# PEER of a one-core decoder layer: the u part first, then v in quarter-feature tiles, with 80 gathered tokens

## The reference, cut to what matters

```
s_top, i_top = lax.top_k(s, PEER_TOPK)                  # per head and half key
best_s, pos = lax.top_k(cand_s, PEER_TOPK)
idx  = ...                                              # (ntok, 128) experts of 16384
gate = softmax(best_s)                                  # (ntok, 128)
act  = gelu(einsum('nd,ned->ne', x, u[idx])) * gate
out  = einsum('ne,ned->nd', act, v[idx])
x    = x + g_c * out ; y = adaLN(RMSNorm(x), c)
```

## Time and profile before

| | us |
|---|---|
| median of 3 runs (lowest, highest) | 2712.4 (2710.21, 2713.03) |
| the profiled execution | 2713.36 |
| its span | 2711.5 |
| busy PE / PEld / DVE / ACT / POOL | 2600.9 / 2400.8 / 1361.7 / 960.9 / 1522.9 |
| HBM read / written | 558.8 / 24.5 MB |

### The profile page before, as it was taken

The page is one execution under the profiler, slowest core; times in us unless marked ns, Lnnn a source line. Parts: engine busy times, 40 slices in busy tenths (PEclk is TensorE's granted clock), DMA queues, the critical chain, the costliest instruction groups (busy, mean ns, idle before and its releaser), DMA issues.

```text
span 2711.5 us, 58935 instructions
## 1 busy us (share of the span) xinstructions
PE 2600.9 (96%) x24221; PEld 2400.8 (89%) x24221; DVE 1361.7 (50%) x2384; ACT 960.9 (35%) x1378; POOL 1522.9 (56%) x724
## 2 busy tenths in 40 slices
PE   5899999889979999999999999999999999999997
PEld 3799999557758999999999988999989999988887
DVE  0540355863236556994576376200676002666566
ACT  1333333341223434444333333333333333333334
POOL 0366676023125776887555544777445776667653
PEclk9899999889978999999999999999999999999999
DMA  9977744587764443445555655555655555888873
GB/s 375 391 282 273 277 158 159 189 286 239 245 221 159 172 164 132 169 155 165 179 188 172 190 185 191 193 183 179 196 186 196 190 180 197 300 324 311 302 272 113
DMA packets 182466, 585.57 MB, mean 216 GB/s; under 512 B 30104, under 2 KB 41000, under 8 KB 153512
## 3 DMA queue, kind: packets, MB, share of 16 engines
q1 hardware_dynamic: 141640, 509.69, 53.6%
q0 software_dynamic: 14672, 55.59, 5.5%
q10 hardware_dynamic: 26000, 18.06, 2.3%
HBM read 558.80 MB, written 24.50 MB: 215 GB/s over the span
## 4 chain that ended last, share of the span: by engine, by line
PE 74%; issue 12%; POOL 10%; DVE 3%; DMA 1%; ACT 0%; POOLq 0%; DVEq 0%; ACTq 0%; SPq 0%
PE bank L905 74%; POOL ring_lo L777 8%; POOL staged L881 1%; POOL ring_lo L784 1%; DVE staged L2860 1%; DMA staged<-late_acts,staged 0%; PE bank L908 0%; DMA staged<-in_w_ada 0%; DVE staged L2336 0%; POOL staged L874 0%; ACT hi_peer L1702 0%; DVE staged L2360 0%; ACT staged L1702 0%; DVE staged L2393 0%; DVE staged L2906 0%
## 5 line engine op out<-in xcount | busy, mean ns | idle before, releaser
L1702 ACT ACTIVATE hi_peer<-kept 128x1024 fp32r<-128x1024 f32 x544 | 546.2, 1052 | 1070.0 <-PE bank L905 1070.0
L777 POOL TENSOR_TENSOR ring_lo<-kept,hi_peer 128x1024 fp32r<-128x1024 f32 x288 | 720.4, 2525 | 279.0 <-ACT hi_peer L1702 279.0
L905 PE MATMUL bank<-h_hi,ring_lo 128*128 128x288 f32 x2848 | 838.0, 294 | 0.0
L905 PE MATMUL bank<-act_hl,hi_peer 128*128 128x248 f32 (+1 forms) x3072 | 706.4, 316 | 4.3 <-POOL ring_lo L784 2.2
L905 PE MATMUL bank<-h_hi,hi_peer 128*128 128x288 f32 x2048 | 608.8, 297 | 2.8 <-POOL ring_lo L777 2.6
L905 PE MATMUL bank<-h_lo,hi_peer 128*128 128x288 f32 x2048 | 604.2, 295 | 0.0
L905 PE MATMUL bank<-act_hl,ring_lo 128*128 128x248 f32 x2048 | 565.4, 276 | 0.0
L905 PEld LDWEIGHTS bank<-act_hl,hi_peer 128*128 128x128 f32 x3072 | 501.7, 188 | 64.5 <-issue 18.9
L905 PEld LDWEIGHTS bank<-h_hi,ring_lo 128*128 128x128 f32 x2848 | 536.6, 188 | 0.0
L784 POOL TENSOR_TENSOR ring_lo<-kept,hi_peer 128x1024 fp32r<-128x1024 f32 (+1 forms) x128 | 264.5, 2066 | 280.0 <-ACT hi_peer L1702 279.3
L905 PE MATMUL bank<-staged 64*64 64x64 f32 (+10 forms) x6520 | 364.4, 284 | 27.5 <-issue 20.0
(11 more groups left out here) (262 smaller groups left out, 2967.3 us busy)
## 6 DMA issues: line engine op xcount, KB each, us to landing
kept<-in_peer_u SPq DMA_DIRECT2D x128, 1024.0 KB, 4.8
kept<-in_peer_v SPq DMA_DIRECT2D x128, 1024.0 KB, 5.7
kept<-in_w_ada SPq DMA_DIRECT2D x64, 1024.0 KB, 8.8
kept<-in_w_in SPq DMA_DIRECT2D x50, 1024.0 KB, 4.8
staged<-in_w_ada SPq DMA_DIRECT2D x32, 1024.0 KB, 6.5
kept<-in_w_adaf SPq DMA_DIRECT2D x32, 1024.0 KB, 5.5
kept<-in_w_out SPq DMA_DIRECT2D x16, 1024.0 KB, 4.8
kept<-in_w_q SPq DMA_DIRECT2D x16, 1024.0 KB, 4.8
```

What stands on the lines that cost most here:

```text
L777: pool.tensor_tensor(ring_lo[:, n % RING_SLOTS, cols], ring[n % RING_SLOTS][:, cols], hi_slot(n)[:, cols].bitcast(F32), ALU.subtract).then ...
L905: return pe.matmul(out, lhsT, rhs, start=start, stop=stop)
L1702: return act.activation(out, in_, ACT.Copy)
```

## The change

The v part comes after all of u, as 128 tiles of four values of b and a quarter of the features (512), in four passes of 8 tiles per quarter; the quarters come in the order 2, 3, 0, 1. `GATHERED` is 80, `VN` 208, and the 40 steps are spread over the 128 tiles. Banks 4 to 7 hold a pass's four 128-feature blocks, each with 2 x 208 columns, so all v tiles have two matmuls per block (416 and 208 columns). GpSimd makes 1024 columns of low weights in every tile and VectorE the other 1024; the cast of the activations moves from VectorE to ScalarE, in two parts of 2 x 208 columns; the first half of a high slot is free at `half_used`. Activations are two buffers of 32 x 208 and one of 32 x 80 for the gathered tokens (`late`), so a u tile has two gelus; `acts` of quarters 0 and 1 are spilled to DRAM and loaded back for the last two. Gates are made for 208 tokens, 52 groups. A pass ends with VectorE's `take_pass`, 8 instructions.

```diff
-GATHERED = 40
+GATHERED = 80
 VN = N - GATHERED
...
+GATE_REST = [min(3, GATE_LAST - at) for at in range(0, GATE_LAST, 3)]
+GATE_TILES = 4 * GATE_BODIES + len(GATE_REST)
+GATE_GROUPS = 12 * GATE_BODIES + GATE_LAST
...
+        segments = [("u", 0), ("u", 1), ("u", 2), ("u", 3), ("v", 2), ("v", 3), ("v", 0), ("v", 1)]
         n_end = n_p + len(segments) * SEG
-        n_v2 = n_p + 6 * SEG
+        n_late = n_p + 4 * SEG
+        LATE_TILES = 4 * SEG
+        V_ORDER = [q for what, q in segments[4:]]
+        PASSES, PASS = 4, SEG // 4
 
...
         def gathered_after(step):
 
-            return 9 + step * 45 // (STEPS - 1)
+            return 9 + step * (LATE_TILES - 19) // (STEPS - 1)
 
...
-        acts = [words(M_ACTS + b * QUARTER * N, QUARTER, N) for b in range(2)]
+        acts = [words(M_ACTS + b * QUARTER * N, QUARTER, VN) for b in range(2)]
+        late = words(M_ACTS + QUARTER * VN, QUARTER, GATHERED)
+        acts_spill = nc.dram_tensor("acts_spill", (2, P, QUARTER, VN), F32, kind="Internal").ap()
...
+
+            def load_acts(q, t):
+
+                own = slice(4 * t, 4 * t + 4)
+                sp.dma_start(acts[q][:, own, :], acts_spill[q][:, own, :]).then_inc(S(f"beside{q}_landed"), 16)
+
+            for m in range(LATE_TILES):
+                n = n_late + m
+                q, at, t = v_place(m)
+                src = v_dram[q * QUARTER + 4 * t:q * QUARTER + 4 * t + 4, :, at * 512:(at + 1) * 512]
+                sp.wait_ge(used, n - RING_SLOTS + 1)
+                sp.dma_start(ring[n % RING_SLOTS].rearrange("p (b d) -> p b d", b=4),
+                             src.rearrange("b a d -> a b d")).then_inc(landed[n % RING_SLOTS], 16)
+                if gates3_at(m + 2) is not None:
+                    load_gates(3, 0, gates3_at(m + 2))
+                if m == SEG:
+                    sp.wait_ge(S("aux_moved"), AUX_MOVED + 32)
+                for b in range(2):
+                    if at == 1 and m // SEG == 1 + b:
+                        if t == 0:
+                            sp.wait_ge(S("acts_split"), 2 * SEG * (1 + b))
+                        load_acts(b, t)
 
...
-            for s, (what, q) in enumerate(segments[:6]):
-                if what == "u":
-                    lo_tiles(n_p + s * SEG, SEG)
-                    continue
-                with pool.Fori(0, SEG // RING_SLOTS) as i:
-                    for j in range(RING_SLOTS):
-                        lo_front(n_p + s * SEG + j, i)
+            for s in range(4):
+                lo_tiles(n_p + s * SEG, SEG)
             v_halves = T["peer_v"].rearrange("e (h d) -> (e h) d", h=2)
-            for m in range(2 * SEG):
-                lo_front(n_v2 + m)
+            for m in range(LATE_TILES):
+                lo_front(n_late + m)
                 if m == 2:
...
 
                 def u_tile(i, j):
                     pe.wait_ge(S("gelu_done"), i * 4 + (q * SEG + j + 1))
-                    if q >= 2:
-                        pe.wait_ge(S("out_taken"), 16 * (q - 1) - 8 + j + 1)
                     dense(n0 + j, h2_hi, h2_lo, i, j)
 
                 if q == 1:
...
+            def v_tile(m):
+
+                first, last = m % PASS == 0, m % PASS == PASS - 1
                 both = first or last
+                turns = [(dt, e) for dt in range(4) for e in range(4)] if both else \
+                    [(dt, e) for e in range(4) for dt in range(4)]
+                pe.wait_ge(S("lo_ready"), lo_halves(n) + 1)
+                pe.wait_ge(S("acts_split"), 2 * m + (2 if both else 1))
                 for dt, e in turns:
+                    if not both and (dt, e) == (0, 2):
+                        pe.wait_ge(S("acts_split"), 2 * m + 2)
+                    if first and e == 0 and m:
+                        pe.wait_ge(S("out_taken"), 4 * (m // PASS - 1) + dt + 1)
+                    cols = slice((e * 4 + dt) * P, (e * 4 + dt + 1) * P)
+                    hi_lo, out = act_hl[:, slot, e, :], ps[4 + dt]
+                    matmul(out[:, 0:2 * VN], w_hi[:, cols], hi_lo, first and e == 0, False)
+                    mm = matmul(out[:, 0:VN], w_lo[:, cols], hi_lo[:, 0:VN], False, last and e == 3)
+                    if last and e == 3 and dt < 3:
...
+            def late_hi(m, part):
+
+                n = n_late + m
+                if m >= 2:
+                    if part == 0:
+                        act.wait_ge(S("half_used"), m - 1)
+                    else:
+                        act.wait_ge(used, n - 1)
+                if part == 0:
+                    act.wait_ge(landed[n % RING_SLOTS], (n // RING_SLOTS + 1) * 16)
+                cols = slice(part * D // 2, (part + 1) * D // 2)
+                copy(hi_slot(n)[:, cols], ring[n % RING_SLOTS][:, cols]).then_inc(S("hi_ready"), 1)
+                late_acts_hi(m, part)
+
+            def late_acts_hi(m, part):
+
+                if part == 0 and m % SEG == 0:
+                    if m < 2 * SEG:
+                        act.wait_ge(S("gates_applied"), 8 * V_ORDER[m // SEG] + 2)
+                    else:
...
+                def tile(i, j, begin=False):
                     act.wait_ge(used, i * 4 + (n0 + j + 1))
+                    hi(n0 + j + 2, i)
+                    if begin:
+                        act.wait_ge(S("side_moved"), 16 + 16 * q)
+                        if q >= 2:
+                            act.wait_ge(S("aux_moved"), AUX_MOVED + 16 * (q - 1))
+                    at = bass.ds(i * 4 + j, 1)
+                    activate(acts[q % 2][:, at, :].rearrange("p o n -> p (o n)"), ps[j % 4][:, 0:VN], ACT.Gelu)
+                    activate(late[:, at, :].rearrange("p o n -> p (o n)"), ps[j % 4][:, VN:N], ACT.Gelu
+                             ).then_inc(S("gelu_done"), 1)
+
+                def spill(b):
+
+                    act.dma_start(acts_spill[b], acts[b]).then_inc(S("aux_moved"), 16)
...
+            def split_acts(m, part):
+
+                n = n_late + m
+                lo, hi = (act_hl[:, n % 2, 2 * part:2 * part + 2, c * VN:(c + 1) * VN] for c in (1, 0))
+                dve.wait_ge(S("acts_hi"), 2 * m + part + 1)
+                ins = tt(lo, acts_part(m, part), hi.bitcast(F32), ALU.subtract)
+                if part == 0:
+                    ins.then_inc(S("acts_split"), 1)
+                    return
                 cols = slice(D // 2, D)
+                dve.wait_ge(S("hi_ready"), 2 * dense_index(n) + part + 1)
                 tt(ring_lo[:, n % RING_SLOTS, cols], ring[n % RING_SLOTS][:, cols], hi_slot(n)[:, cols].bitcast(F32),
+                   ALU.subtract).then_inc(S("acts_split"), 1)
...
+            def take_pass(p):
+
+                for dt in range(4):
+                    k_ = 4 * p + dt
+                    if k_:
+                        dve.wait_ge(S("out_taken"), k_)
+                    if dt < 3:
+                        dve.wait_ge(S("v_sum"), 3 * p + dt + 1)
                     else:
...
+
+            for m in range(LATE_TILES):
+                if m >= 2 * SEG and m % SEG == 0:
+                    dve.wait_ge(S(f"beside{V_ORDER[m // SEG]}_landed"), EARLY_LANDED + 16 * PASS)
+                for side in range(2):
+                    split_acts(m, side)
+                if m == 1:
+                    dve.wait_ge(S("gelu_done"), 4 * SEG + 4)
+                    link(dve.memset(spread_acts, 0.0))
+                late_work(m)
+                if gates3_at(m) is not None:
+                    apply_gates(3, gates3_at(m) // 2, gates3_at(m) % 2)
+                if m and m % PASS == 0:
+                    take_pass(m // PASS - 1)
+            link(stt(out=gain3, in0=mods[:, SC_F], scalar=1.0, in1=over(prm("gfin"), 2, NS), op0=ALU.add, op1=ALU.mult))
+            dve.sem_inc(S("final_step"), 1)
+            take_pass(LATE_TILES // PASS - 1)
```

More of the change, by code:

```diff
@@ L520, in dense_index, with v_place, acts_part, gates3_at @@
             return n - n_z if n < n_ada1 else n - n_wo + 50
[L522 to L525 removed]
+        def v_place(m):
+            return V_ORDER[m // SEG], m % SEG // PASS, m % PASS
+        def acts_part(m, part):
+            q, _, t = v_place(m)
+            return acts[q % 2][:, 4 * t + 2 * part:4 * t + 2 * part + 2, :]
+        def gates3_at(m):
+            return (m - 2) // 3 if m % 3 == 2 and m < 24 else None
         def hi_slot(n):
@@ new lines, in _ @@
+                    spill(1)
+                    with act.Fori(SEG // 4 - 2, SEG // 4) as i:
+                        for j in range(4):
+                            tile(i, j)
+                else:
+                    for j in range(4):
+                        tile(0, j, j == 0)
+                    with act.Fori(1, SEG // 4 - 1) as i:
+                        for j in range(4):
+                            tile(i, j)
+                    for j in range(4):
+                        tile(SEG // 4 - 1, j)
+                        if j >= 2:
+                            for part in range(2):
+                                late_acts_hi(j - 2, part)
```

(1 more changed line is left out.)

360 lines of the change are left out of this document (114 added, 246 removed).

## The result

| | before | after |
|---|---|---|
| median, us (lowest, highest) | 2712.7 (2710.21, 2713.03) | 2779.7 (2766.74, 2787.93) |
| profiled execution, us | 2713.36 | 2766.74 |
| its span, us | 2711.5 | 2764.9 |
| span from the start of v work to the end of it, us | 755.9 (four windows) | 816.8 |

The changed kernel takes 1.0243 of the time before, 95% interval 1.0223 to 1.0262: 2.4% slower, where 0.6% faster was forecast. (The median before is that of four executions.) The profiled execution is the fastest of the four of the changed kernel ("after" from here on), so the profile shows 13 us less than the median.

The account below looks back on a forecast made before the run. TensorE, 98 to 100% busy, was taken as the bound. 2711.5 span - 9.1 gates - 755.9 old v + 698.3 new v + 42 GpSimd + 6 pass ends + 3 gate products = 2695.8, giving 2697 us; range 2668 to 2728.

Parts of the forecast that it names:

- The gates: u quarter making gate products: 52 instead of 62 groups at 0.91 us each, -9.1 us.
- TensorE's own v time: v part: 614.4 dense tiles (4.80 each) + 80.4 steps + 3.5 `turn_late` = 698.3 us, against 755.9 before.
- the rival of hidden loads: Dense v tiles: 208-column matmuls take 0.097 us, tile 4.56; total 2681, or 2670 with stalls at lower bound; chance 0.18.
- The sign named for it: Late v tile: next matmul 0.112 us after a 208-column one starts, or 0.097 if loads are hidden.
- u quarters 2 and 3, ScalarE's two gelus, spills, tail: u part and end: u quarters stay 204.8 us; gelus, spills, reloads cost 0; tail the same length.
- VectorE's part: v part: 6 us for takes at pass boundaries plus 3 for quarter 3's gate products; work per tile less than before.
- the pass ends: 15 pass boundaries: VectorE's takes from PSUM delay TensorE 0.4 us each, 6 us, bounds 0 and 22.
- Late weights: v tile loads in 2 KB pieces land late; at 0.4 us per step the gain is gone, 2712; chance 0.12.
- GpSimd's stalls: v part: low weights late behind gathers, 2.1 us per pair of steps, 20 pairs, 42 us; bounds 22 and 142.
- its break-even: Stalls in the v part that cancel the gain: 67 us against 51 forecast, 3.4 a pair of steps.
- the rival that names it: v part: GpSimd becomes the bound; stalls 151 us, time 2797, about 2740 half-way; chance 0.20.
- the upper bound: GpSimd in v part: every operation meets one of VectorE's, 7.1 us a pair of steps, 142 us.

Follow-up runs that it names:

- e9: Changed kernel, but the low weights' matmul of every v block streams 176 or 240 columns instead of 208: 2769.57 and 2770.94 us, one execution each.
- e3: Changed kernel without row gathers on GpSimd; SyncE loads fixed blocks of rows of the same size instead: 2672.33 us, ratio 0.9848.
- e6: Changed kernel with each pair of row gathers one tile later, behind the low weights TensorE needs next: 2706.7 us, ratio 0.9971.
- e2: Changed kernel with VectorE's 1024 columns of low weights made before its second activation split instead of after: 2744.34 us, ratio 1.0118.
- e1: Changed kernel, but GpSimd makes only 640 columns of low weights per v tile and VectorE 384 more: 2698.22 us, ratio 0.9939.
- e11: Changed kernel with row gathers one tile later and GpSimd making 512 columns of low weights, VectorE the rest: 2678.64 us, ratio 0.9856.
- e4: Changed kernel with 64 gathered tokens instead of 80, so 32 steps and dense v for 224 tokens: 2738.98 us, ratio 1.0084.
- e5: Changed kernel with 640 columns on GpSimd and VectorE's low weights ahead of its second split, gathers unmoved: 2695.02 us, ratio 0.993.
- e8: Changed kernel with row gathers one tile later and VectorE's low weights ahead of its second split: 2703.07 us, ratio 0.9959.
- e7: Changed kernel with row gathers one tile later and 640 columns of low weights on GpSimd: 2682.79 us, ratio 0.989.

## Why the prediction was wrong

**The gates, right.** -9.1 forecast; 261.2 to 252.3 is -8.9.

**TensorE's own v time, right.** A late tile without gathers is 4.81 us (4.80 forecast), a step 2.04 (2.01), and the rival of hidden loads (4.56) is refuted, by the tile and by the two runs above. The sign named for it, 0.112 from the short matmul's start to the next, isn't in the records: within a pair the starts are 0.21 and 0.09 apart, and it is their sum and the starts of the loads (e9) that show the floor. `turn_late` took 4.6 instead of 3.5.

**u quarters 2 and 3, ScalarE's two gelus, spills, tail: right.** 204.8 each; the tail is 17.8 us against 18.0.

**VectorE's part, right in size by luck.** TensorE waits 4.6 + 2.8 us for it, against 6 for the pass ends and 3 for the gate products. But none of these waits is at a pass end: the first tile of a pass takes 4.79 to 4.81 us wherever it isn't the second or third after a step, so the 6 should have been 0. The 4.6 are three waits in the fifth to seventh v tile, for splits of 3.32, 2.44 and 2.43 us where an undisturbed one is 0.58. Each of the three runs beside GpSimd's operation on low weights and ends 0.45 us after it, the last at 1964.77 and 1964.32: the collision again, with VectorE as the one held up. VectorE's work per tile, said to be less than before, rose to 4.61 us.

**Late weights, refuted** as the cause, by e3. v tiles do land later, 7.4 us after their start at the median instead of 5.7, and ScalarE waits 28.7 us for ten of them. They become the next limit once GpSimd is out of the way (74 to 111 us of waits on ScalarE in e3 and e6).

**GpSimd's stalls: the step that failed.** The mechanism stood in the prediction, with its break-even of 3.4 us a pair of steps (2.9, if the 9 us of VectorE are taken off the 67) and its sign of GpSimd three quarters busy (614.8/816.8 = 75%). Its size was taken as 2.1, 42 us in all, and the rival that names it, between half-way (2740 there; half of the way from 2697 to 2797 is 2747) and full price (2797), was given 0.20. The median of 2779.7 lies in it.

By the ends of the tiles, where steps stand three tiles apart, the second and third tile after a step with an activation gather are 0.93 and 2.37 late, without one 1.21 and 1.58: 6.1 a pair, with the slow stretches of the clock in it. Of the 118.5 us, 7 are waits for VectorE, 1 is `turn_late`'s, about 13 are the clock's (below), and some 97 are left against 42. This is by subtraction: 2.5 of the 97 are the 0.01 of a tile and the 0.03 of a step, 75.3 are TensorE's waits for GpSimd on record, and the rest is named by no wait. The working also priced pairs of steps only. The fourth to eighth v tile, ahead of the first step, where the first eight row gathers and four activation gathers are started, take 10.6 us more than five tiles of 4.81. Without these and the clock a pair costs some 4.5 us, between the 2.1 taken and the 7.1 of the upper bound.

Why 2.1 was wrong: "With 0.03 on each row gather" took a row gather at the 0.97 of v quarter 3 of before, and with it a VectorE that is somewhere else when the gather starts. The change itself puts VectorE there. The cast moved to ScalarE, so VectorE's splits wait for ScalarE's two copies (L2777 sat idle 216 us for them), and its 1024 columns now start at 2.05 after the tile's end in the step shown, where the gather starts at 2.13. An average was carried over where the working had all it needed to place both instructions: copies 1.05 and 0.5 after the tile's end, splits, then the low weights; it even did so for the pass ends.

The row gather measured 1.276. With it, the measured operation (2.435) and activation gather (1.237), the prediction's own chain gives 2.8 late with and 1.3 without an activation gather, 4.1 a pair and 81 us. That is 39 of the 55 us between 42 and 97, nearly all by the row gather.

The Trainium skill ("SBUF — State Buffer", section "SBUF: two separate sides") says that whichever of VectorE and GpSimd starts first holds their shared ports for a whole instruction, but that a VectorE operation with two inputs in SBUF does so only against a GpSimd operation that reads SBUF. The gather of 1.95, which ends 0.81 after VectorE's operation does (2390.23 against 2389.42), looks like such a lock; that starting a gather counts as such a read is not shown. The upper bound, 142 us, took every operation as held, and at 97 measured it was hardly nearer than the 42 taken.

The collision is not the larger part, though. The slack of 0.09 us at the first operation (6.72 against 6.81) was a forecast of none, and "just in time" was counted as free; what lengthened the instructions ahead went straight to TensorE, as the 1.03 us of the step shown do. e2 takes the collision away and gains 35 us (23 in the v part); e1 leaves it and gives the queue slack, and gains 81.5 (65). e6 gains 73 (65) by both.

**The forecast time.** 2697 + (97 - 42) + 13 + 1 - 2 is about 2764, against 2766.7 of the profiled execution; the median is 13 higher. The mean granted clock is 0.969, 0.964, 0.965 and 0.959 over the four executions of 2766.74, 2777.16, 2782.25 and 2787.93 us, so the slower ones had less of it. Where isn't known: it can be more of the stretches told of below, or the part ahead of v, which differs by 15 us between e2 and e11 at the same code. The kernel before varies in the same way, 2707.87 us at 0.978 to 2717.38 at 0.971.

## What to carry to other kernels

When an engine's operation grows in an in-order queue that also holds DMA starts behind a wait, place every instruction of the queue and of the engine that shares its ports on one time axis for one period, and count slack near zero as a loss. First try the order: put the operation that TensorE needs next ahead of the gathers (73 us here), and leave the engine with the wait the smaller share of the work (81.5 us; 97 with both), before giving up the larger change. And give a stall that grows with the queue's load its whole range of prices; its middle was worth more than the 0.20 it got.

## What was not expected of the hardware

In the v part of after the granted clock falls to about half, the 1.2 GHz level, eight times, each for 3.4 us and each soon after TensorE had waited 1.7 to 2.6 us for GpSimd; before, it was 1.00 in all four v windows. The first such stretch and its neighbours, with the columns of the earlier trace rows:

```profile
1966.00:1974.00 8.00, 5.40 (x36) 5.12 (x35) 5.66 (x6) 4.50 (x7) 7.37 (x5) 0.99 0.86 278
1974.00:1977.40 3.40, 3.40 (x14) 3.30 (x13) 3.40 (x3) 0.00 (x0) 0.81 (x1) 0.52 0.20 76
1977.40:1981.00 3.60, 3.60 (x25) 3.59 (x25) 3.38 (x8) 2.38 (x4) 1.24 (x1) 1.00 0.09 16
```

and TensorE ahead of it and in it:

```profile
1972.54 0.46 PE L927 MATMUL bank<-act_hl,hi_peer 128*128 128x416 f32 x1 [2.60 <-POOL ring_lo L811]
...
1974.37 0.59 PE L927 MATMUL bank<-act_hl,hi_peer 128*128 128x416 f32 x1
...
1974.93 0.59 PE L927 MATMUL bank<-act_hl,hi_peer 128*128 128x416 f32 x1
```

A pair takes 0.56 us instead of 0.30, and a stretch costs about 1.7 us: a stall of 2 us is paid nearly twice where the clock follows it. Eight are some 13 us. The other kernels have fewer, by and large in the order of their stalls: e2 seven, e4 six (counting a stretch of 6.8 us as two), e5, e6 and e8 five, e1 three, e3 and e11 two, e7 one (the two of e9, with stalls like after's, have twelve and eight). So some of what the edits gained is the clock's. Of the 18 waits for GpSimd of over 1.5 us in after's v part, ten were followed by none, the longest (2.9, at 2039.90) among them; what sets the eight apart is not shown.
